# Attention in an inference step: where the value product stands among the transposes

## The chip, the cores and the metric

The kernel runs on one NeuronCore of a Trainium2 chip. The metric is the device time of one execution in microseconds (us), the median of the runs shown. The engines that matter are TensorE (PE in the profile; its weight loads are PEld), VectorE (DVE), ScalarE (ACT), GpSimd (POOL) and SyncE (SP), which issues transfers.

## What is computed

The reference is one step of a layer: modulated RMS norm, one projection into three head groups, their output projection, and a mixture of 16 experts. The change concerns the third head group, latent attention. Cut to that:

```python
q = jnp.einsum('bnr,rf->bnf', rmsnorm(c_q, q_norm_g), w_qb)      # 8 heads of 64 + 32
k, v = mla_keys_values(all_ckv, all_krope, w_kvb)                # k: 96 wide, v: 64 wide
s  = jnp.einsum('bqhd,bkhd->bhqk', qi, k).astype(jnp.float32) * ATTN_SCALE
pr = jax.nn.softmax(s, axis=-1).astype(v.dtype)
o  = jnp.einsum('bhqk,bkhd->bqhd', pr, v)
```

There are 1024 sample tokens, whose 8 query tiles of 128 see 1280 keys (1024 of their own and 256 cached), and 128 prompt tokens, one query tile that sees 128 keys. Everything is float32.

## The kernel before, in words

The program is written by hand, engine by engine, with semaphores; no scheduler moves anything. Attention takes 4 rounds, `i` = 0 to 3, of two heads each. The first three rounds are one loop body, the last is written out again with other filling work.

In a round, a **job** `n` is one head's 128 queries: token tile `t = n // 2`, head `j = n % 2` of the round. Jobs 0 to 15 have 1280 keys, jobs 16 and 17 (the prompt) 128. A job with an even number is called an even query here, the one behind it the odd query of the same tile. A job passes these steps:

- `score(i, n, ch)` (L711, TensorE): three matmuls, for 512, 512 and 256 keys, into PSUM banks 0 to 2 for an even job and 3 to 5 for an odd one. The first waits for `exp_ok` of job `n - 2`, which had the same banks.
- `highest` (L1554, VectorE): the maximum over the 1280 scores, and behind it the negated maximum (L1556).
- `exponential` (L1222, ScalarE): the exponential into `prob[n % 2]`, with its sum.
- `scaled` (L1575 and L1577, VectorE): reciprocal of the sum, and the row scaled by it. It posts `norm_ok`.
- `turn(n, ch)` (L753, TensorE): transposes of the probabilities, 4, 4 and 2 tiles of 128 for `ch` = 0, 1, 2, into PSUM banks 6 and 7 in turn. The first waits for `norm_ok`.
- `turned` (L1210 on ScalarE; L1588 on VectorE for chunk 0 of odd jobs, the list `DVE_TURNS`): these banks copied into `probT`.
- `weigh(t)` (L768, TensorE): the value product of both heads of tile `t`, 20 matmuls with an output of 64 rows each. It needs all chunks of `probT` of job `2t + 1`.
- `weighed` (L1568, VectorE): its result copied out. It posts `pv_out`.

TensorE's order is the Python loop in `attend` (two jobs to a step of `n`, called a **period** in this document). VectorE's order in a period is `highest(n)`, `turned(n - 1)`, `highest(n + 1)`, `scaled(n)`, `weighed((n - 2) // 2)`, `scaled(n + 1)`; in three periods of each of the first three rounds (`n` = 4, 6, 8) `fold_wq` (L1398, L1402) follows, a third of the next round's query weights each time. ScalarE's order is `turned(n - 2, 2)`, `exponential(n)`, `turned(n - 1, 1)`, `turned(n - 1, 2)`, `exponential(n + 1)`, `turned(n, 0)`, `turned(n, 1)`.

Banks 6 and 7 go round by the list `MID_ORDER`, which must name the turns and the value products in TensorE's order: entry number `at` uses bank `6 + at % 2`, and `bank_free` makes each wait until the entry two places before it is copied out. After job 15, the tail of a round mixes the last turns with `fill(x)`: the next round's `queries` (L681), or in the last round `out_proj` (L821).

Behind a round come the next two heads' keys and values (`keys_values`: L722, L694), and behind attention the rest of the output projection, the router and the experts (L1058, L1082), which take more than half of the time.

Of the kernel before, what the change touches and what calls it, by code (L numbers as in the profile page):

```python
# [131 lines left out]
def build(nc, x_prompt, x_sample, cache_ckv, cache_krope, c, c_ctx, w_ada, b_ada, norm1_g, norm2_g,  # L132
# [9 lines left out]
    with ctx:  # L142
# [232 lines left out]
        def pv_at(t):  # L375
            return bank[MID_BANK[("weigh", t)]][:, 0:P]

        def turn_out(eng, i, n, ch):

            if (n, ch) in DVE_TURNS:  # L380
                eng.wait_ge(t_out_d, i * len(DVE_TURNS) + DVE_TURNS.index((n, ch)) + 1)
            else:
                eng.wait_ge(t_out, i * len(ACT_TURNS) + ACT_TURNS.index((n, ch)) + 1)
# [148 lines left out]
        def _(pe):  # L532
# [22 lines left out]
            for n, job in enumerate(JOBS):  # L555
# [75 lines left out]
                elif kind == "gate":  # L631

                    m, g = job[1], job[2]
# [8 lines left out]
                elif kind == "pool":  # L642
                    m, g = job[1], job[2]
# [54 lines left out]
            def score(i, n, ch):  # L698

                t, j = divmod(n, 2)  # L700
                if n == 0:
                    pe.wait_ge(k_out, i * 3 + ch + 1)
                if n == 1 and ch == 0:
                    pe.wait_ge(q_out, i * 6 + 6)
                if n >= 2 and ch == 0:
                    pe.wait_ge(exp_ok, i * 18 + n - 1)
                if t < NT - 1:
                    k0, kn = ((0, 512), (512, 512), (1024, 256))[ch]
                else:
                    k0, kn = KEYS, NPR  # L710
                mm = pe.matmul(bank[3 * (n % 2) + ch][:, 0:kn], qT[:, j, t * P:(t + 1) * P], kT[:, j, k0:k0 + kn],  # L711
                               start=True, stop=True)
                if ch == 2 or t == NT - 1:
                    mm.then_inc(s_mm, 1)
# [19 lines left out]
            def attend(i, fill):  # L734

                def bank_free(user):

                    at = MID_ORDER.index(user)
                    if at < 2:
                        pe.wait_ge(v_out, i * 3 + 2 + at)  # L740
                    elif MID_ORDER[at - 2][0] == "turn":
                        turn_out(pe, i, *MID_ORDER[at - 2][1:])
                    else:
                        pe.wait_ge(pv_out, i * NT + MID_ORDER[at - 2][1] + 1)

                def turn(n, ch):

                    if ch == 0:
                        pe.wait_ge(norm_ok, i * 18 + n + 1)
                    bank_free(("turn", n, ch))  # L750
                    for a in range(CHUNK_TILES[ch] if n < 16 else 1):
                        kt = 4 * ch + a
                        mm = pe.transpose(bank[MID_BANK[("turn", n, ch)]][:, a * P:(a + 1) * P],  # L753
                                          prob[n % 2][:, kt * P:(kt + 1) * P], ident)
                    mm.then_inc(t_mm, 1)

                def weigh(t):

                    if t < 7:
                        turn_out(pe, i, 2 * t + 1, 0)  # L760
                    turn_out(pe, i, 2 * t + 1, 1 if t < NT - 1 else 0)
                    bank_free(("weigh", t))
                    for kt in range(10) if t < NT - 1 else range(10, 11):
                        if kt == 8:
                            turn_out(pe, i, 2 * t + 1, 2)
                        for j in range(2):
                            src = kt if t < NT - 1 else 0
                            mm = pe.matmul(pv_at(t)[64 * j:64 * j + 64, :], v_sb[:, kt, 64 * j:64 * j + 64],  # L768
                                           probT[:, 2 * (t % 2) + j, src * P:(src + 1) * P],
                                           start=(kt in (0, 10)), stop=(kt in (9, 10)))  # L770
                    mm.then_inc(pv_mm, 1)

                for n in range(2, 16, 2):
                    if n >= 4:
                        weigh((n - 4) // 2)
                    score(i, n, 0)
                    score(i, n, 1)
                    turn(n - 2, 0)
                    score(i, n, 2)
                    turn(n - 2, 1)  # L780
                    turn(n - 2, 2)
                    for ch in range(3):
                        score(i, n + 1, ch)
                        turn(n - 1, ch)
                weigh(6)
                score(i, 16, 0)
                fill(0)
                turn(14, 0)
                turn(14, 1)
                score(i, 17, 0)  # L790
                fill(1)
                turn(14, 2)
                turn(15, 0)
                fill(2)
                turn(15, 1)
                turn(15, 2)
                fill(3)
                turn(16, 0)
                turn(17, 0)
                weigh(7)  # L800
                fill(4)
                weigh(8)
                fill(5)
# [25 lines left out]
            with pe.Fori(0, 3) as i:  # L829
                attend(i, lambda x: queries(i + 1, x))  # L830
                keys_values(i + 1)
            attend(3, lambda x: out_proj(x) if x < 4 else None)


# [1299 lines left out]
def turns_before(n, ch):  # L2134
# [4 lines left out]
DVE_TURNS = [(n, 0) for n in range(1, 15, 2)]  # L2139
ACT_TURNS = [(n, ch) for n in range(18) for ch in range(3 if n < 16 else 1) if (n, ch) not in DVE_TURNS]  # L2140

MID_ORDER = [u for n in range(0, 14, 2) for u in [("weigh", (n - 2) // 2)][:n // 2]
             + [("turn", m, ch) for m in (n, n + 1) for ch in range(3)]]
MID_ORDER += [("weigh", 6)] + [("turn", n, ch) for n in (14, 15) for ch in range(3)]
MID_ORDER += [("turn", 16, 0), ("turn", 17, 0), ("weigh", 7), ("weigh", 8)]
MID_BANK = {u: 6 + at % 2 for at, u in enumerate(MID_ORDER)}

# [30 lines left out]
```

## Time and profile before

| | |
|---|---|
| median of 3 runs | 1656.54 us (1655.87 to 1659.05) |
| the profiled execution's own time | 1657.21 us |
| its span | 1655.2 us |
| PE busy | 1586.8 us (96%) |
| PEld busy | 1265.9 us (76%) |
| DVE busy | 551.5 us (33%) |
| ACT busy | 416.2 us (25%) |
| mean granted TensorE clock | 0.989 |

The span is what the profiler saw on the core; the execution's own time is 2.0 us longer, and the profiled execution was 0.7 us above the median. Matmuls are pipelined: the records of one group overlap, and the time a group takes is read from the start of one group to the start of the next. A float32 matmul leaves two records, a transpose one.

### The profile page before, as it was taken

How to read it: one execution, taken by the hardware profiler on the slowest of the kernel's cores; microseconds unless marked ns; L12 is line 12 of the kernel's file. 1: busy time of each engine (PE TensorE's matmuls, PEld its weight loads, DVE VectorE, ACT ScalarE, POOL GpSimd, SP SyncE). 2: the span in 40 equal slices, each digit the busy share in tenths (PEclk: the TensorE clock that was granted, in tenths of full speed). 3: DMA queues.
4: the chain of work that ended last, by engine and by line, in shares of the span. 5: the costliest groups of instructions: out<-in, count | busy, mean ns of one | idle time of the engine just before them, and what ended most of it. 6: DMA issues, size and time to landing. Idle time of an engine off the chain costs nothing.

```text
span 1655.2 us, 26952 instructions
## 1 busy us (share of the span) xinstructions
PE 1586.8 (96%) x10945; PEld 1265.9 (76%) x10945; DVE 551.5 (33%) x1315; ACT 416.2 (25%) x944; POOL 107.6 (7%) x109
## 2 busy tenths in 40 slices
PE   4899998999999999999879999999999999999997
PEld 3645444666667666544469999999999999999996
DVE  3101333474746646214477111111111111111114
ACT  4200101354545545233411111111111111111114
POOL 0004400000000000021100100000000000000010
PEclk9999999999999999999979999999999999999999
DMA  7861002200000000061149777878777878777776
GB/s 303 327 240 72 0 0 95 72 1 12 2 0 13 0 5 1 3 242 62 77 142 365 271 271 287 288 271 303 257 270 276 310 259 301 269 274 265 282 229 242
DMA packets 113514, 288.05 MB, mean 174 GB/s; under 512 B 10095, under 2 KB 15126, under 8 KB 110254
## 3 DMA queue, kind: packets, MB, share of 16 engines
q1 hardware_dynamic: 108702, 269.88, 44.3%
q0 software_dynamic: 4752, 17.30, 3.9%
q8 instruction: 45, 0.74, 0.2%
q14 instruction: 15, 0.12, 0.0%
HBM read 265.53 MB, written 21.64 MB: 174 GB/s over the span
## 4 chain that ended last, share of the span: by engine, by line
PE 94%; DVE 3%; DMA 1%; ACT 1%; issue 1%; SPq 0%; DVEq 0%
PE ps L1058 30%; PE ps L1082 15%; PE ps L711 9%; PE ps L537 9%; PE ps L821 7%; PE ps L768 5%; PE ps L753 4%; PE ps L681 3%; PE ps L598 2%; PE ps L694 1%; PE ps L722 1%; PE ps L550 1%; DVE hreg L1714 1%; PE ps L629 1%; PE ps L1013 1%; PE ps L1021 1%
## 5 line engine op out<-in xcount | busy, mean ns | idle before, releaser
L1058 PE MATMUL ps<-mreg,wreg 128*128 128x144 f32 x4096 | 517.9, 287 | 0.0
L1058 PEld LDWEIGHTS ps<-mreg,wreg 128*128 128x128 f32 x4096 | 509.7, 190 | 0.5 <-issue 0.4
L1082 PE MATMUL ps<-mreg,wreg 128*128 128x144 f32 x2048 | 265.5, 286 | 0.0
L1082 PEld LDWEIGHTS ps<-mreg,wreg 128*128 128x128 f32 x2048 | 258.0, 190 | 0.0
L1919 DVE TENSOR_TENSOR mreg<-ps,mreg 128x144 f32<-128x144 f32 x120 | 36.9, 307 | 443.0 <-PE ps L1058 443.0
L711 PE MATMUL ps<-wreg 128*128 128x512 f32 (+2 forms) x400 | 167.9, 519 | 0.0
L1344 ACT ACTIVATE mreg<-ps 128x144 f32<-128x144 f32 x128 | 37.1, 290 | 445.7 <-PE ps L1058 445.7
L537 PE MATMUL ps<-hreg,wreg 128*128 128x512 f32 (+1 forms) x432 | 143.2, 489 | 0.0
L821 PE MATMUL ps<-wreg,mreg 128*128 128x512 f32 x288 | 130.4, 598 | 2.6 <-DVE wreg L1635 2.6
L1554 DVE TENSOR_REDUCE stat<-ps 128x1 f32<-128x1280 f32 (+1 forms) x72 | 97.7, 1357 | 90.9 <-PE ps L711 90.9
L753 PEld LDWEIGHTS ps<-const,hreg 128*128 128x128 f32 x648 | 80.0, 141 | 58.3 <-issue 38.9
L537 PEld LDWEIGHTS ps<-hreg,wreg 128*128 128x128 f32 x432 | 70.7, 191 | 70.0 <-issue 69.6
L1210 ACT ACTIVATE hreg<-ps 128x512 f32<-128x512 f32 (+2 forms) x172 | 82.1, 501 | 109.9 <-PE ps L753 107.7
L1894 DVE TENSOR_SCALAR mreg<-ps,gain,modT 128x128 f32<-128x128 f32 x128 | 51.8, 408 | 160.2 <-PE ps L1013 160.0
L1222 ACT ACTIVATE hreg<-ps,stat 128x1280 f32<-128x1280 f32 (+1 forms) x72 | 88.0, 1222 | 68.3 <-DVE stat L1556 68.3
L1348 ACT ACTIVATE mreg<-ps,modT 128x128 f32<-128x128 f32 x128 | 47.0, 367 | 224.7 <-PE ps L1082 224.6
L753 PE MATMUL ps<-const,hreg 128*128 128x128 f32 x648 | 97.2, 274 | 0.0
L821 PEld LDWEIGHTS ps<-wreg,mreg 128*128 128x128 f32 x288 | 52.1, 190 | 57.8 <-issue 57.8
L711 PEld LDWEIGHTS ps<-wreg 128*128 128x128 f32 x400 | 64.0, 190 | 26.9 <-issue 24.9
L768 PE MATMUL ps<-hreg,wreg 128*64 128x128 f32 x1296 | 78.5, 275 | 4.6 <-ACT hreg L1210 1.1
L768 PEld LDWEIGHTS ps<-hreg,wreg 128*64 128x64 f32 x1296 | 70.9, 137 | 13.7 <-ACT hreg L1210 9.1
L1577 DVE TENSOR_SCALAR hreg<-hreg,stat 128x1280 f32<-128x1280 f32 (+1 forms) x72 | 59.0, 820 | 2.5
(254 smaller groups left out, 1174.1 us busy)
## 6 DMA issues: line engine op xcount, KB each, us to landing
wreg<-in_w_e_dram SPq DMA_DIRECT2D x96, 2048.0 KB, 12.2
wreg<-in_w_ada_dram SPq DMA_DIRECT2D x24, 1024.0 KB, 10.1
out_dram<-wreg SPq DMA_DIRECT2D x9, 512.0 KB, 2.6
mreg<-in_x_sample_dram SPq DMA_DIRECT2D x8, 512.0 KB, 8.3
wreg<-in_w_out_dram SPq DMA_DIRECT2D x1, 4096.0 KB, 13.4
wreg<-in_x_sample_dram SPq DMA_DIRECT2D x8, 512.0 KB, 6.0
x_rows<-wreg SPq DMA_DIRECT2D x8, 512.0 KB, 2.8
xn_rows<-wreg SPq DMA_DIRECT2D x8, 512.0 KB, 2.7
```

The costliest lines, as they stand in the source:

```text
L537: mm = pe.matmul(bank[n % 8][:, 0:gn], w_in_sb[:, k, w_at + m * P:w_at + (m + 1) * P], hT[:, k, g0:g0 + gn], start=(k == 0), stop=(k == KD ...
L711: mm = pe.matmul(bank[3 * (n % 2) + ch][:, 0:kn], qT[:, j, t * P:(t + 1) * P], kT[:, j, k0:k0 + kn], start=True, stop=True)
L753: mm = pe.transpose(bank[MID_BANK[("turn", n, ch)]][:, a * P:(a + 1) * P], prob[n % 2][:, kt * P:(kt + 1) * P], ident)
L768: mm = pe.matmul(pv_at(t)[64 * j:64 * j + 64, :], v_sb[:, kt, 64 * j:64 * j + 64], probT[:, 2 * (t % 2) + j, src * P:(src + 1) * P], start ...
L821: mm = pe.matmul(bank[o_bank(x)], mixT[:, k, t * P:(t + 1) * P], w_out_sb[:, k, hf * 512:(hf + 1) * 512], start=(k == 0), stop=(k == KD - 1))
L1058: mm = pe.matmul(o[:, 0:CAP], w[s][:, k, (f % 4) * P:(f % 4 + 1) * P], xsT[b][:, k, :], start=(k == 0), stop=(k == KD - 1))
L1082: mm = pe.matmul(bank[4 + dm % 2][:, 0:CAP], w2[f // 4][:, f % 4, dm * P:(dm + 1) * P], hidT[:, f, :], start=(f == 0), stop=(f == 7))
L1210: act.activation(probT[:, 2 * (t % 2) + j, ch * 512:ch * 512 + w], bank[MID_BANK[("turn", n, ch)]][:, 0:w], ACT.Copy).then_inc(t_out, 1)
L1222: act.activation(prob[n % 2][:, 0:w], src, ACT.Exp, bias=a_neg[:, n % 4:n % 4 + 1], scale=SCALE, accum_out=a_sum[:, n % 4:n % 4 + 1]).then ...
L1554: dve.tensor_reduce(a_max[:, r:r + 1], src, AX_X, ALU.max).then_inc(max_ok, 1)
L1577: dve.tensor_scalar(prob[n % 2][:, 0:w], prob[n % 2][:, 0:w], a_rec[:, r:r + 1], None, ALU.mult).then_inc(norm_ok, 1)
L1894: dve.tensor_scalar(xsT[b][:, k, 0:CAPS], bank[6 + k % 2][:, 0:CAPS], gain2[:, 0, k:k + 1], modT[:, 0, 24 + k:25 + k], ALU.mult, ALU.add). ...
```

## The change

Two places change together. In TensorE's loop, `weigh` moves from ahead of a period's scores to behind `score(i, n, 2)`, so that it stands after chunk 0 of the even query's transposes and ahead of chunks 1 and 2. The last one, `weigh(6)`, moves from ahead of `score(i, 16, 0)` to behind `turn(14, 0)`. `MID_ORDER` follows, so the bank of each entry and the entry it waits for change too. The orders of VectorE, ScalarE, GpSimd and SyncE do not change.

```diff
                 for n in range(2, 16, 2):
-                    if n >= 4:
-                        weigh((n - 4) // 2)
                     score(i, n, 0)
                     score(i, n, 1)
                     turn(n - 2, 0)
                     score(i, n, 2)
+                    if n >= 4:
+                        weigh((n - 4) // 2)
                     turn(n - 2, 1)
                     turn(n - 2, 2)
                     for ch in range(3):
                         score(i, n + 1, ch)
                         turn(n - 1, ch)
-                weigh(6)
                 score(i, 16, 0)
                 fill(0)
                 turn(14, 0)
+                weigh(6)
                 turn(14, 1)
...
-MID_ORDER = [u for n in range(0, 14, 2) for u in [("weigh", (n - 2) // 2)][:n // 2]
-             + [("turn", m, ch) for m in (n, n + 1) for ch in range(3)]]
-MID_ORDER += [("weigh", 6)] + [("turn", n, ch) for n in (14, 15) for ch in range(3)]
+MID_ORDER = [u for n in range(0, 16, 2)
+             for u in [("turn", n, 0)] + [("weigh", (n - 2) // 2)][:n // 2] + [("turn", n, 1), ("turn", n, 2)]
+             + [("turn", n + 1, ch) for ch in range(3)]]
```

TensorE, one period of the last round, before. L768 is the value product, L711 the scores, L753 the transposes:

```order
350 L768 MATMUL ps<-hreg,wreg 64x128 x20
351 L711 MATMUL ps<-wreg 128x512 x2
352 L753 MATMUL ps<-const,hreg 128x128 x4
353 L711 MATMUL ps<-wreg 128x256
354 L753 MATMUL ps<-const,hreg 128x128 x6
355 L711 MATMUL ps<-wreg 128x512
356 L753 MATMUL ps<-const,hreg 128x128 x4
357 L711 MATMUL ps<-wreg 128x512
358 L753 MATMUL ps<-const,hreg 128x128 x4
359 L711 MATMUL ps<-wreg 128x256
360 L753 MATMUL ps<-const,hreg 128x128 x2
```

and the same period now:

```order
343 L711 MATMUL ps<-wreg 128x512 x2
344 L753 MATMUL ps<-const,hreg 128x128 x4
345 L711 MATMUL ps<-wreg 128x256
346 L768 MATMUL ps<-hreg,wreg 64x128 x20
347 L753 MATMUL ps<-const,hreg 128x128 x6
348 L711 MATMUL ps<-wreg 128x512
349 L753 MATMUL ps<-const,hreg 128x128 x4
350 L711 MATMUL ps<-wreg 128x512
351 L753 MATMUL ps<-const,hreg 128x128 x4
352 L711 MATMUL ps<-wreg 128x256
353 L753 MATMUL ps<-const,hreg 128x128 x2
```

The 20 matmuls of the value product have passed three score matmuls and the four transposes of the even query's chunk 0; nothing else has changed places.

TensorE, the tail of the last round (L821 is the output projection that fills there), as the difference:

```order
 L711 MATMUL ps<-wreg 128x128
 L821 MATMUL ps<-wreg,mreg 128x512 x8
-L753 MATMUL ps<-const,hreg 128x128 x8
+L753 MATMUL ps<-const,hreg 128x128 x4
+L768 MATMUL ps<-hreg,wreg 64x128 x20
+L753 MATMUL ps<-const,hreg 128x128 x4
 L711 MATMUL ps<-wreg 128x128
 L821 MATMUL ps<-wreg,mreg 128x512 x8
```

`weigh(6)` now stands between the two chunks of job 14, behind a whole piece of filling work.

VectorE, one period of the last round, which is the same before and now (L1554 and L1556 are `highest`, L1588 `turned`, L1575 and L1577 `scaled`, L1568 `weighed`; in the first three rounds `fold_wq` follows in three periods):

```order
273 L1554 TENSOR_REDUCE stat<-ps 128x1
274 L1556 TENSOR_SCALAR stat<-stat 128x1
275 L1588 COPY hreg<-ps 128x512
276 L1554 TENSOR_REDUCE stat<-ps 128x1
277 L1556 TENSOR_SCALAR stat<-stat 128x1
278 L1575 RECIPROCAL stat<-stat 128x1
279 L1577 TENSOR_SCALAR hreg<-hreg,stat 128x1280
280 L1568 COPY mreg<-ps 128x128
281 L1575 RECIPROCAL stat<-stat 128x1
282 L1577 TENSOR_SCALAR hreg<-hreg,stat 128x1280
```

The copy of the value product (L1568) stays where it was, between the scaling of the even query and that of the odd one.

## Rows read from the trace of the kernel before

**Rows 1.** The page: busy time and instructions of each engine, and the chain's engines.

```profile
PE 1586.8 (96%) x10945; PEld 1265.9 (76%) x10945; DVE 551.5 (33%) x1315; ACT 416.2 (25%) x944; POOL 107.6 (7%) x109
...
PE 94%; DVE 3%; DMA 1%; ACT 1%; issue 1%; SPq 0%; DVEq 0%
```

**Rows 2.** Timeline of PE, one period: start us, us, what [idle before]; later pieces left out.

```profile
338.39 0.38 PE L753 MATMUL ps<-const,hreg 128*128 128x128 f32 x2
338.90 2.40 PE L768 MATMUL ps<-hreg,wreg 128*64 128x128 f32 x40
341.23 1.98 PE L711 MATMUL ps<-wreg 128*128 128x512 f32 x4
343.06 0.60 PE L753 MATMUL ps<-const,hreg 128*128 128x128 f32 x4
...
343.93 0.85 PE L753 MATMUL ps<-const,hreg 128*128 128x128 f32 x6
344.62 1.02 PE L711 MATMUL ps<-wreg 128*128 128x512 f32 x2
...
347.64 0.38 PE L753 MATMUL ps<-const,hreg 128*128 128x128 f32 x2
```

**Rows 3.** Windows of one period: length, busy us of PE, PEld, DVE, ACT, POOL, clock, DMA.

```profile
338.90:348.15 9.25, 9.13 (x72) 6.43 (x73) 6.80 (x14) 5.28 (x10) 0.00 (x0) 1.00 0.01 2
```

**Rows 4.** Line 768: what it waited for and who waited for it (us, times).

```profile
  ACT hreg L1210: 10.2, 29
...
  DVE mreg L1568: 19.2, 25
```

**Rows 5.** Timeline of PEld, the value product's weight loads in the same period.

```profile
338.87 2.19 PEld L768 LDWEIGHTS ps<-hreg,wreg 128*64 128x64 f32 x40 [0.33 <-ACT hreg L1210]
```

**Rows 6.** Timeline of ACT in the same period.

```profile
338.16 1.03 ACT L1210 ACTIVATE hreg<-ps 128x512 f32<-128x512 f32 x2 [0.15 <-PE ps L753]
340.31 1.33 ACT L1222 ACTIVATE hreg<-ps,stat 128x1280 f32<-128x1280 f32 x1 [1.11 <-DVE stat L1556]
341.53 0.19 ACT L1222 ACTIVATION_READ_ACCUMULATOR hreg<-ps,stat 128x1 f32 x1
343.69 0.60 ACT L1210 ACTIVATE hreg<-ps 128x512 f32<-128x512 f32 x1 [1.97 <-PE ps L753]
```

**Rows 7.** Timeline of DVE in the same period.

```profile
338.59 1.49 DVE L1554 TENSOR_REDUCE stat<-ps 128x1 f32<-128x1280 f32 x1 [1.04 <-PE ps L711]
...
340.19 0.15 DVE L1575 RECIPROCAL stat<-stat 128x1 f32<-128x1 f32 x1
340.38 0.89 DVE L1577 TENSOR_SCALAR hreg<-hreg,stat 128x1280 f32<-128x1280 f32 x1
341.45 0.29 DVE L1568 COPY mreg<-ps 128x128 f32 x1 [0.18 <-PE ps L768]
341.76 0.16 DVE L1575 RECIPROCAL stat<-stat 128x1 f32<-128x1 f32 x1
341.95 0.89 DVE L1577 TENSOR_SCALAR hreg<-hreg,stat 128x1280 f32<-128x1280 f32 x1
342.76 0.32 DVE L1398 TENSOR_SCALAR hreg<-hreg,vT 128x192 f32<-128x192 f32 x1
342.99 0.38 DVE L1402 TENSOR_SCALAR hreg<-hreg,vT 128x32 f32<-128x32 f32 x2
344.13 1.49 DVE L1554 TENSOR_REDUCE stat<-ps 128x1 f32<-128x1280 f32 x1 [0.76 <-PE ps L711]
...
346.11 0.69 DVE L1588 COPY hreg<-ps 128x512 f32<-128x512 f32 x1 [0.31 <-PE ps L753]
```

**Rows 8.** Timeline of PE ahead of attention: a piece behind a long wait.

```profile
282.64 0.76 PE L653 MATMUL ps<-const,wreg 128*128 128x128 f32 x4 [2.34 <-DVE wreg L1516]
```

**Rows 9.** Windows, the columns as in rows 3, PEclk behind POOL's.

```profile
280.00:290.00 10.00, 6.47 (x16) 3.27 (x16) 5.26 (x17) 2.88 (x7) 0.00 (x0) 0.66 0.96 344
700.00:710.00 10.00, 7.40 (x46) 4.08 (x42) 4.57 (x14) 2.63 (x4) 4.66 (x2) 1.00 0.71 259
```

## Prediction

> **What bounds the kernel now.** I read the page first: TensorE is busy 96% of the span, and 94% of the chain that ended last lies on it [rows 1]. So what TensorE waits for counts one for one, and what the others wait for costs nothing until TensorE waits for them. Next the timeline of one period of attention on TensorE. The value product starts at 338.90 and again at 348.15, 9.25 us later [rows 2, 3]. Inside a period the pieces start one behind the other, with one hole: the last two transposes of the odd query start at 338.39 and stream for 0.23 us (six take 343.93 to 344.62, 0.69 us), so TensorE is free at 338.62, and the value product starts at 338.90. That is 0.28 us. The waits of its line say for what: ScalarE's copies, 29 times, 10.2 us in all, 0.35 us each [rows 4]. The copy of chunk 1 starts at 338.16 and takes 0.60 us, to 338.76, and the weight load follows at 338.87 [rows 5, 6]. So a result is handed to TensorE in 0.11 us.
>
> Then VectorE over the same period. It is busy 6.80 of 9.25 us [rows 3], never late, and its order is fixed. `highest` of the odd query starts at 338.59, 0.20 us behind the start of the transposes at 338.39; `scaled` of the even query ends at 340.38 + 0.89 = 341.27; the value product's copy runs at 341.45, with only 0.18 us of waiting ahead of it; `scaled` of the odd query follows, then `fold_wq` to 342.99 + 0.38 = 343.37 [rows 7]. All of this lies behind the 2.33 us of the value product and the 1.83 us of the two scores behind it (338.90, 341.23, 343.06) [rows 2]. The even query's probabilities are ready at 341.27 and first transposed at 343.06: 1.79 us of room, less 0.11.
>
> **The change, step by step.** No instruction is added or removed; no transfer moves. TensorE gets three score matmuls and four transposes ahead of the value product, and the place of VectorE's copy of it stays.
>
> *What is saved.* The 0.28 us hole: between the odd query's last transposes and the value product lie now at least 1.83 + 0.87 us of work (341.23 to 343.06, then 343.06 to 343.93) [rows 2], and ScalarE is done in 0.5. Over 7 value products in 4 rounds this is 28 x 0.28 = 7.8 us, if nothing else happens.
>
> *What is added first.* The even query's transposes now come 2.33 us sooner after the odd scores. TensorE, free at 338.62, would start the two scores at once and end them at 338.62 + 1.83 = 340.45, while the probabilities come at 341.27 + 0.11 = 341.38. It waits 0.93 us. Net of the hole: +0.65.
>
> *What is added next, and is larger.* VectorE takes things in order, and the copy of the value product stands ahead of `scaled` of the odd query and of `highest` of the next even query. Before, it waited 0.18 us for that product. Now the product cannot start before the transposes of chunk 0, which cannot start before `scaled` of the even query. VectorE has to stand idle for 0.11 + 0.87 (chunk 0 and the third score) + 2.55 (product start 338.90 to copy start 341.45) = 3.53 us from its own `scaled` to its own copy, where it stood 0.18. Its idle time in a period was only 9.25 - 6.80 = 2.45 us, so it becomes a part of the loop that sets the period. Two closed loops result; each is a sum of steps from [rows 2, 7].
>
> Loop A, with `fold_wq`, lies on VectorE but for the product: `highest` to the next instruction 1.60 (338.59 to 340.19), `turned` 0.69, `highest` of the odd query 1.60, reciprocal and scaling of the even one 1.08 (340.19 to 341.27), hand-over 0.11, transposes and third score 0.87, product up to its copy 2.55, copy 0.31 (341.45 to 341.76), scaling of the odd one 1.00 (to 342.76), folding 0.61 (to 343.37). Sum **10.42 us**. Without the folding it is 9.81, and the other loop rules.
>
> Loop B goes through TensorE: product 2.55, copy 0.29 and hand-over 0.11 (chunk 2 of the even query takes the product's bank and waits for its copy), two transposes 0.23, the odd query's scores with the transposes between them 3.02 (344.62 to 347.64), 0.20 to `highest`, 1.60, 1.08, 0.11, 0.87. Sum **10.06 us**.
>
> Against 9.25 that is +1.17 us in a period with folding and +0.81 without. ScalarE's exponential of the even query, 3.13 us from `highest` to its end (338.59 to 341.53 + 0.19, the same for both) [rows 6, 7], also comes late, and the next scores wait some 0.6 us for it; but the transposes behind them wait for VectorE anyway, so the wait only takes part of theirs.
>
> *The sum.* A round has 7 large value products. Its first full period pays the +0.65 above; five intervals between products follow, three of them with folding in rounds 0 to 2: 3 x 1.17 + 2 x 0.81 = 5.13. At the tail, job 16's scores wait about 0.6 us for job 14's exponential, less the hole of 0.28 and some overlap: I take +0.25, an estimate between 0 and 0.6. The filling projections there hide the rest. Round: 5.13 + 0.65 + 0.25 = 6.03. The last round does not fold: 5 x 0.81 + 0.90 = 4.95. Sum 3 x 6.03 + 4.95 = **23.0 us**. On the profiled execution's 1657.2 us this gives 1680.2; that execution was 0.7 above the median, so I say **1679.5 us**, 1.4% slower.
>
> *Bounds.* From below: back to back, VectorE's instructions overlap by 0.08 us (342.76 against 341.95 + 0.89), which could shorten each of the eight steps of loop A a little, to 9.9, where loop B holds it; then all periods cost 0.81 less some hundredths and the sum is near 17. From above: each hand-over to TensorE may expose twice the 0.11, one more in loop A and two in loop B, 28 x 0.2 = 6 us, and the tail may pay all of its 0.6, 1.4 us more: 30.
>
> **A rule weighed.** In the period, weight loads fill 6.43 of 9.25 us, 70%, and VectorE 6.80, 74% [rows 3]: by these shares neither is full. The Trainium skill, "Perfetto Trace Analysis", section "Identifying the Most-Contended Engine", says to judge TensorE's headroom by the weight loads' share rather than by matmul busy time, and VectorE's by its share. By that reading both have a quarter to spare, the order would not matter and the sum would be zero. I take the starts of the pieces instead, since they follow each other with 0.28 us free in 9.25.
>
> **The rivals.**
>
> 1. *Faster.* The hole goes and nothing takes its place. This needs the even query's probabilities on TensorE's side at 340.45 at the latest in the time of the rows, 0.93 us sooner than they come; from there on the sign turns. Then 28 x 0.28 = 7.8 us go: 1648.7. For it: VectorE idles 2.45 us in a period. Against: the idle time lies ahead of steps that need TensorE's scores, not where it could be used. 0.05.
> 2. *No change.* The slack of VectorE (2.45 us) takes in the added wait, and TensorE's hole and wait cancel: within 3 us of 1656.5. The rule above is its best argument; the closed loops speak against it, since they leave no slack. 0.04.
> 3. *Waits in series.* The late exponential (0.6 us) is not absorbed but adds to the loop, each period: 28 x 0.6 = 17 on top of 23, so 1696. It would need chunk 0's transposes to follow the scores without waiting. 0.08.
> 4. *The clock falls.* Before attention, TensorE waited 2.34 us in one piece [rows 8], and in these 10 us its granted clock was 0.66, so part of them ran at the lower of its two levels (1.2 and 2.4 GHz). But in 700 to 710 it was busy only 7.40 us of 10 at 1.00, and a forecast period is busy at least 8.5 of 10 [rows 9]. If every period ran at 0.66, 34% of some 290 us would come on top, about 98: near 1777. The Trainium skill, "TensorE: Matmul & The Clock Gate", section "A second HAM failure mode: psum-queue depth-cycling", describes just such short idle times between groups of matmuls setting the clock back and forth. 0.02.
>
> My forecast has 0.81.
>
> **How the numbers follow.** The forecast's own range is 1656.5 + 17 - 2 for small things not seen, to 1656.5 + 30 + 3: 1671 to 1690. Rivals 1, 2 and 4 and most of 3 lie outside, 0.19, so the range of 8 in 10 is just this one. A measurement of this kernel can tell about 0.2%, 3.3 us, from no change. Faster takes rival 1, 0.05; same rival 2, 0.04; slower the rest, 0.91.
>
> **What would show it.** Right: value products 10.4 us apart in the folding periods, 10.06 in others; about 3.5 us of idle time ahead of each copy on line 1568, so that its wait for line 768 grows from 19.2 us [rows 4] to near 100; TensorE's line 753 waiting for VectorE's line 1577 and for the product's copy, line 711 for ScalarE's line 1222; the wait of line 768 for ScalarE down from 10.2 us to about 1; the clock at 1.00; everything behind attention unchanged in length. Wrong: products 9.0 us apart (rival 1) or 9.25 (rival 2); a wait of 0.6 us ahead of the scores with a full 1 us still ahead of the transposes (rival 3); a granted clock below 1.00 between 310 and 730 us (rival 4).

## The result and the profile after

The changed kernel takes **1682.32 us** (median of 4 runs, 1681.56 to 1684.86), the kernel before 1657.36 (4 runs, 1655.87 to 1659.05). The ratio is 1.0153, with a 95% interval of 1.0141 to 1.0165: 1.5% slower, 25 us. The forecast was 1679.5, between 1671 and 1690.

The page of the changed kernel, to be held against [rows 1]:

```profile
PE 1598.5 (95%) x10945; PEld 1258.8 (75%) x10945; DVE 543.9 (32%) x1315; ACT 411.9 (25%) x944; POOL 107.8 (6%) x109
...
PE 88%; DVE 8%; issue 2%; DMA 1%; ACT 1%; SPq 0%; DVEq 0%; ACTq 0%
```

The instructions are as many as before, and TensorE is about as busy. What moved is the chain: 94% on TensorE has become 88%, and VectorE has gone from 3% to 8%. VectorE, busy a third of the span, is now in part what the end waits for.

All of the loss is in attention. I call **attention** the stretch from the first matmul on line 722 (the first round's keys) to the end of the last value product. It goes from 300.59 to 724.68 + 2.62 = 727.30 us, which is 426.71 us, by the changed kernel's timeline of PE:

```profile
300.59 0.59 PE L722 MATMUL ps<-creg,share 128*128 128x512 f32 x1
...
724.68 2.62 PE L768 MATMUL ps<-hreg,wreg 128*64 128x128 f32 x44 [0.35 <-ACT hreg L1210]
```

The same two places of the kernel before lie at 299.64 and 701.69: 402.05 us. The difference is 24.66. Behind attention it is 953.50 us against 953.51.

The waits of line 768 and those of the two engines it feeds. First who waited for the value product, and for whom it waited, against [rows 4]:

```profile
  issue: 10.9, 31
  ACT hreg L1210: 3.2, 8
who waited for it (us, times):
  DVE mreg L1568: 122.8, 32
```

VectorE's copy now waits 122.8 us for it instead of 19.2. And the waits of attention, 310 to 730 us (engine and line, whom it waited for: us, times, longest):

```profile
PEld ps L711 <- ACT hreg L1222: 14.3, 24, 0.6
...
PEld ps L753 <- DVE hreg L1577: 10.0, 12, 1.7
PE ps L711 <- ACT hreg L1222: 8.6, 24, 0.4
PEld ps L753 <- DVE hreg L1588: 6.6, 13, 0.7
PE ps L753 <- DVE hreg L1577: 6.4, 15, 0.9
...
PEld ps L753 <- DVE mreg L1568: 2.5, 16, 0.2
```

None of these waits stood there before: scores for the exponential, transposes for the scaled probabilities, for `turned`, and for the value product's copy. One period with folding on TensorE, from product to product (345.43 to 355.73, 10.30 us, where [rows 2, 3] have 9.25):

```profile
345.43 2.40 PE L768 MATMUL ps<-hreg,wreg 128*64 128x128 f32 x40
347.76 1.01 PE L753 MATMUL ps<-const,hreg 128*128 128x128 f32 x6
348.61 1.02 PE L711 MATMUL ps<-wreg 128*128 128x512 f32 x2
...
352.07 0.44 PE L753 MATMUL ps<-const,hreg 128*128 128x128 f32 x2 [0.27 <-DVE hreg L1588]
352.88 1.98 PE L711 MATMUL ps<-wreg 128*128 128x512 f32 x4 [0.38 <-ACT hreg L1222]
354.72 0.65 PE L753 MATMUL ps<-const,hreg 128*128 128x128 f32 x4
...
355.73 2.40 PE L768 MATMUL ps<-hreg,wreg 128*64 128x128 f32 x40
```

and on VectorE, against [rows 7]:

```profile
339.39 1.49 DVE L1554 TENSOR_REDUCE stat<-ps 128x1 f32<-128x1280 f32 x1
...
341.01 0.69 DVE L1588 COPY hreg<-ps 128x512 f32<-128x512 f32 x1
341.62 1.48 DVE L1554 TENSOR_REDUCE stat<-ps 128x1 f32<-128x1280 f32 x1
...
343.21 0.15 DVE L1575 RECIPROCAL stat<-stat 128x1 f32<-128x1 f32 x1
343.39 0.89 DVE L1577 TENSOR_SCALAR hreg<-hreg,stat 128x1280 f32<-128x1280 f32 x1
347.98 0.29 DVE L1568 COPY mreg<-ps 128x128 f32 x1 [3.70 <-PE ps L768]
348.19 0.15 DVE L1575 RECIPROCAL stat<-stat 128x1 f32<-128x1 f32 x1
348.38 0.89 DVE L1577 TENSOR_SCALAR hreg<-hreg,stat 128x1280 f32<-128x1280 f32 x1
349.18 0.32 DVE L1398 TENSOR_SCALAR hreg<-hreg,vT 128x192 f32<-128x192 f32 x1
...
349.70 1.48 DVE L1554 TENSOR_REDUCE stat<-ps 128x1 f32<-128x1280 f32 x1
```

The reader should see loop A here: VectorE goes from `highest` at 339.39 to `highest` at 349.70 without one idle moment of its own but the 3.70 us ahead of the copy. Before, a folding period had waits for scores of 0.76 and 1.04 us. From `highest` of the even query to the transposes a second way of equal length runs beside VectorE's: through ScalarE's exponential and the scores that wait for it (`<-ACT hreg L1222` above). e11 shows what follows from that.

### The profile page after: what moved, and what is told of

The parts are those of the page before. It is cut to its first block, busy times and chain, and to the rows that moved or that the text cites. A ratio compares the mean times of both kernels' runs of the same rounds, so it can differ in the third digit from the quotient of the medians.

```text
span 1680.8 us, 26931 instructions
## 1 busy us (share of the span) xinstructions
PE 1598.5 (95%) x10945; PEld 1258.8 (75%) x10945; DVE 543.9 (32%) x1315; ACT 411.9 (25%) x944; POOL 107.8 (6%) x109
## 4 chain that ended last, share of the span: by engine, by line
PE 88%; DVE 8%; issue 2%; DMA 1%; ACT 1%; SPq 0%; DVEq 0%; ACTq 0%
PE ps L1058 30%; PE ps L1082 14%; PE ps L537 8%; PE ps L821 7%; PE ps L711 5%; PE ps L768 5%; PE ps L753 3%; PE ps L681 3%; DVE stat L1554 2%; PE ps L598 2%; PE ps L694 1%; PE ps L722 1%; PE ps L550 1%; DVE hreg L1714 1%; PE ps L629 1%
## 5 line engine op out<-in xcount | busy, mean ns | idle before, releaser
L711 PE MATMUL ps<-wreg 128*128 128x512 f32 (+2 forms) x400 | 167.5, 518 | 8.6 <-ACT hreg L1222 8.6
L753 PEld LDWEIGHTS ps<-const,hreg 128*128 128x128 f32 x648 | 73.6, 141 | 81.5 <-issue 46.2
L821 PE MATMUL ps<-wreg,mreg 128*128 128x512 f32 x288 | 130.4, 598 | 2.6 <-DVE wreg L1635 2.6
L753 PE MATMUL ps<-const,hreg 128*128 128x128 f32 x648 | 103.1, 280 | 8.8 <-DVE hreg L1577 6.4
L1554 DVE TENSOR_REDUCE stat<-ps 128x1 f32<-128x1280 f32 (+1 forms) x72 | 97.4, 1353 | 37.5 <-PE ps L711 37.5
L1222 ACT ACTIVATE hreg<-ps,stat 128x1280 f32<-128x1280 f32 (+1 forms) x72 | 87.9, 1221 | 81.1 <-DVE stat L1556 80.7
L821 PEld LDWEIGHTS ps<-wreg,mreg 128*128 128x128 f32 x288 | 52.1, 190 | 57.8 <-issue 57.8
L711 PEld LDWEIGHTS ps<-wreg 128*128 128x128 f32 x400 | 64.0, 190 | 36.4 <-issue 20.1
L768 PEld LDWEIGHTS ps<-hreg,wreg 128*64 128x64 f32 x1296 | 70.0, 137 | 12.9 <-issue 10.9
L768 PE MATMUL ps<-hreg,wreg 128*64 128x128 f32 x1296 | 78.5, 275 | 1.1 <-ACT hreg L1210 1.1
L1577 DVE TENSOR_SCALAR hreg<-hreg,stat 128x1280 f32<-128x1280 f32 (+1 forms) x72 | 59.0, 820 | 2.6
## 6 DMA issues: line engine op xcount, KB each, us to landing
wreg<-in_w_ada_dram SPq DMA_DIRECT2D x24, 1024.0 KB, 10.3
```

The costliest lines, as they stand in the source:

```text
L821: mm = pe.matmul(bank[o_bank(x)], mixT[:, k, t * P:(t + 1) * P], w_out_sb[:, k, hf * 512:(hf + 1) * 512], start=(k == 0), stop=(k == KD - 1))
L1222: act.activation(prob[n % 2][:, 0:w], src, ACT.Exp, bias=a_neg[:, n % 4:n % 4 + 1], scale=SCALE, accum_out=a_sum[:, n % 4:n % 4 + 1]).then ...
L1554: dve.tensor_reduce(a_max[:, r:r + 1], src, AX_X, ALU.max).then_inc(max_ok, 1)
L1577: dve.tensor_scalar(prob[n % 2][:, 0:w], prob[n % 2][:, 0:w], a_rec[:, r:r + 1], None, ALU.mult).then_inc(norm_ok, 1)
```

## The experiments

Eleven kernels were run, each beside runs of the kernel before on its own chip (medians 1657.11 us for e1 to e4, 1657.75 for e5 to e8, 1657.06 for e9 to e11). The table has the two measures: the whole (ratio to the kernel before, with its interval) and attention alone, from the profile of each kernel. Attention is the sharper one. The stretch ahead of it, which no edit touches, ended between 297.7 and 303.4 us in the profiles, and a spread of that size is in the totals too; behind attention the profiles have 952.6 to 955.2 us (e8 apart). Attention came out at 402.05, 402.04 and 402.09 us in the three kernels whose TensorE order is that of the kernel before.

| kernel | median us | ratio | attention us | to before | products apart, us: without folding / with / last round |
|---|---|---|---|---|---|
| before | 1657.36 | | 402.05 | | 9.25 / 9.25 / 9.25 |
| after | 1682.32 | 1.0153 (1.0141 to 1.0165) | 426.71 | +24.66 | 10.25 / 10.31 / 10.05 |
| e1_first_score | 1654.10 | 0.9984 (0.9976 to 0.9993) | 397.39 | -4.66 | 9.06 / 9.06 / 9.06 |
| e2_tail_only | 1660.01 | 1.0012 (1.0003 to 1.0020) | 401.20 | -0.85 | 9.25 / 9.25 / 9.25 |
| e3_vector_order | 1656.12 | 0.9990 (0.9981 to 0.9999) | 398.37 | -3.68 | 9.12 / 9.25 / 9.01 |
| e4_copy_later | 1679.14 | 1.0135 (1.0120 to 1.0149) | 423.64 | +21.59 | 10.24 / 10.23 / 10.05 |
| e5_two_scores | 1656.72 | 0.9993 (0.9984 to 1.0002) | 399.62 | -2.43 | 9.01 / 9.37 / 9.01 |
| e6_after_more_vector | 1685.26 | 1.0162 (1.0147 to 1.0178) | 429.77 | +27.72 | 10.25 / 10.65 / 10.05 |
| e7_before_more_vector | 1658.04 | 0.9999 (0.9989 to 1.0008) | 402.04 | -0.01 | 9.25 / 9.25 / 9.25 |
| e8_after_unrolled | 1731.21 | 1.0445 (1.0430 to 1.0459) | 425.70 | +23.65 | 10.17 / 10.24 / 10.05 |
| e9_before_vector_order | 1658.02 | 1.0006 (0.9996 to 1.0015) | 402.09 | +0.04 | 9.25 / 9.25 / 9.25 |
| e10_first_score_and_tail | 1652.54 | 0.9978 (0.9968 to 0.9988) | 396.57 | -5.48 | 9.06 / 9.06 / 9.06 |
| e11_scaled_first | 1673.64 | 1.0098 (1.0082 to 1.0113) | 416.46 | +14.41 | 9.73 / 10.25 / 9.61 |

**Half of the change's way.** The value product behind one score matmul, where nothing of the even query's transposes is passed:

```diff
                 for n in range(2, 16, 2):
-                    if n >= 4:
-                        weigh((n - 4) // 2)
                     score(i, n, 0)
+                    if n >= 4:
+                        weigh((n - 4) // 2)
                     score(i, n, 1)
                     turn(n - 2, 0)
```

> The kernel before, with the value product one score matmul later: behind score(i, n, 0) instead of ahead of it; the tail and the bank order stay. Theory (the loop through VectorE, entered because the even query's probabilities come too late): their scaling has room here, since the product and a score still lie ahead of the transposes, so only the 0.28 us hole goes: products 8.97 us apart, some 7 to 8 us off the whole, ratio 0.995. Rival A (any step of the value product away from its place costs on TensorE, by switching between kinds of matmul or by the bank order): same or slower than before. Rival B (only the late exponential matters): as the theory here.

The products stand 9.06 us apart and attention is 4.66 us shorter, so rival A falls: moving the product does not by itself make the kernel slower. Of the hole of 0.28 us, 0.19 came back as time. The timeline of PE shows the rest:

```profile
334.37 1.02 PE L711 MATMUL ps<-wreg 128*128 128x512 f32 x2
335.23 0.60 PE L753 MATMUL ps<-const,hreg 128*128 128x128 f32 x4
...
336.10 0.38 PE L753 MATMUL ps<-const,hreg 128*128 128x128 f32 x2
336.32 1.02 PE L711 MATMUL ps<-wreg 128*128 128x512 f32 x2
337.27 2.40 PE L768 MATMUL ps<-hreg,wreg 128*64 128x128 f32 x40
339.61 1.12 PE L711 MATMUL ps<-wreg 128*128 128x512 f32 x2
340.57 0.60 PE L753 MATMUL ps<-const,hreg 128*128 128x128 f32 x4
```

The scores follow the transposes at once (336.32), but the product starts 0.95 us behind the start of a score that streams for 0.86 elsewhere (334.37 to 335.23), and the score behind the product takes 0.96 (339.61 to 340.57). The steps from score to product and from product to score cost some 0.1 us each here, and the first of them is new. That is also why less came than was expected: six products of a round move here, not seven, and 24 x 0.19 = 4.6 us. The median gained 3.0 us of the 7 to 8 that were expected.

**The tail alone.** The loop and its banks as before; only this, and the last entries of `MID_ORDER` in step:

```diff
-                weigh(6)
                 score(i, 16, 0)
                 fill(0)
                 turn(14, 0)
+                weigh(6)
                 turn(14, 1)
```

> Only the second half of the change: weigh(6) behind turn(14, 0), the loop's periods as before. Theory: the tail has filling work of the next projections on TensorE, so nothing waits; one hole of 0.28 us a round goes, about -1 us in all, within the noise. Then the whole cost of the change is that of the loop. Rival (the tail carries a good part of the 25 us): +3 us or more.

Attention is 0.85 us shorter, as expected. The whole came out 0.12% longer, and its runs fell in two groups, three near 1656.5 and eight near 1660.5 us. The profiled one, of the second group, entered attention at 302.44 us, 2.80 later than the profiled run of the kernel before, and needed 1.7 us more behind it (955.2 against 953.5). Neither stretch was edited, and no experiment here explains why this kernel's runs are mostly the longer ones. The tail has no part in the 24.66 us.

**VectorE's order.** TensorE as in the change. On VectorE, this:

```diff
                     highest(i, n)
                     turned(n - 1)
+                    scaled(n)
                     highest(i, n + 1)
-                    scaled(n)
-                    weighed((n - 2) // 2)
                     scaled(n + 1)
+                    weighed((n - 2) // 2)
```

> The changed kernel, TensorE's order and banks as changed; VectorE's order alone is another: scaled(n) ahead of highest(n + 1), and the value product's copy behind scaled(n + 1). Theory: the even query's probabilities come 1.6 us sooner, and nothing of VectorE stands behind the product but its own copy, so both loops open: products about 9.0 us apart without folding and 9.3 with it, the whole 3 to 7 us faster than the kernel before, ratio 0.996 to 0.998. Rival A (the new place costs on TensorE itself, or by its banks): it stays 20 to 25 us slower. Rival B (the exponential's lateness sets the loop): in between, 10 us slower or more.

In attention the 24.66 us are gone and 3.68 with them; the whole is 1.0 us below the kernel before (0.9990), where 3 to 7 were expected. This is the strongest result: TensorE issues the very order of the changed kernel, so neither its order nor its banks make the loss by themselves. The last round of this kernel on VectorE:

```profile
617.19 0.89 DVE L1577 TENSOR_SCALAR hreg<-hreg,stat 128x1280 f32<-128x1280 f32 x1
617.99 1.49 DVE L1554 TENSOR_REDUCE stat<-ps 128x1 f32<-128x1280 f32 x1
...
621.35 0.89 DVE L1577 TENSOR_SCALAR hreg<-hreg,stat 128x1280 f32<-128x1280 f32 x1
622.63 0.29 DVE L1568 COPY mreg<-ps 128x128 f32<-128x128 f32 x1 [0.39 <-PE ps L768]
622.84 1.48 DVE L1554 TENSOR_REDUCE stat<-ps 128x1 f32<-128x1280 f32 x1
```

The even query is scaled at 617.19, ahead of the odd query's maximum, and the copy waits 0.39 us, where it waits 3.53 in the last round of the changed kernel. TensorE's products are 9.01 us apart.

**One half of it, the copy.** The changed kernel with only the value product's copy moved:

```diff
                     scaled(n)
-                    weighed((n - 2) // 2)
                     scaled(n + 1)
+                    weighed((n - 2) // 2)
```

> The changed kernel with half of that: only the value product's copy behind scaled(n + 1) on VectorE, highest(n + 1) still ahead of scaled(n). Theory: loop A (through VectorE's own order) opens and loop B (product, copy, bank, odd scores, highest, scaling of the even query, transposes) stays: products 10.05 us apart in folding periods too, +16 to +19 us to the kernel before, 6 to 9 less than the change. Rival (VectorE's stall ahead of the copy is all of it): near the time of the kernel before.

Products are 10.23 us apart in folding periods too: loop A is open, loop B stands. Attention is 3.1 us shorter than the change's, not 6 to 9, because loop B is longer in the looped rounds (10.23) than the 10.05 expected and found in the last one; e8 takes that up. Of the 3.1 us, 0.75 lie in the five intervals of the looped rounds (51.17 us a round instead of 51.42) and some 2.3 in the interval behind the sixth product (9.79 instead of 10.37). The rival falls: VectorE's stall ahead of the copy was not all of it.

**The other half.** The copy stays ahead of `scaled(n + 1)`:

```diff
+                    scaled(n)
                     highest(i, n + 1)
-                    scaled(n)
                     weighed((n - 2) // 2)
```

> The changed kernel with the other half of the VectorE edit alone: scaled(n) ahead of highest(n + 1), the value product's copy still ahead of scaled(n + 1). Theory: loop B opens (the probabilities no longer wait for the maximum of the odd query), loop A stays in another form, from the copy through scaled(n + 1), highest of the next even query, its exponential, its scaling, the transposes and the product: 9.7 to 9.9 us without folding and about 10.3 with it, +12 to +16 us to the kernel before. Rival (each half takes away its own share of the cost, so that they add): 21.6 of 24.7 us stay with the first half alone, so this one would have to end near the kernel before.

9.61 to 9.73 us without folding and 10.25 with it, +14.41: loop B is open, another form of loop A is left. It runs through ScalarE's exponential of the even query and the two scores behind it. In a folding period of this kernel the even query is scaled at 342.77 + 0.89 = 343.66, and the transposes start only at 344.41, behind scores that waited for the exponential:

```profile
342.59 1.98 PE L711 MATMUL ps<-wreg 128*128 128x512 f32 x4 [0.38 <-ACT hreg L1222]
344.41 0.60 PE L753 MATMUL ps<-const,hreg 128*128 128x128 f32 x4
```

So with folding the way through VectorE's own steps and the way through the exponential are nearly equal: taking the first away made the period only 0.06 us shorter (10.31 to 10.25). The late exponential, rival B of e3, is thus the second branch of loop A; e3 opens both, since from the product's end to the even query's `highest` only the copy and the folding are left there. The two halves take away 3.1 and 10.3 us of the change's cost alone, 28.3 together. They are two loops over the same period, and the period is as long as the longer one.

**VectorE's order with TensorE's old one.** The two moves of e3, made in the kernel before:

```diff
+                    scaled(n)
                     highest(i, n + 1)
-                    scaled(n)
-                    weighed((n - 2) // 2)
                     scaled(n + 1)
+                    weighed((n - 2) // 2)
```

> The kernel before with the VectorE order of the run that undid the cost (scaled(n) ahead of highest(n + 1), the copy behind scaled(n + 1)); TensorE as before. A control. Theory: with TensorE's old order no loop runs through VectorE, so this order is worth nothing by itself: products 9.25 us apart, attention within 0.5 us of the kernel before. Rival (that VectorE order is simply the better one, and its gain hid a cost of TensorE's new order): 4 us faster or more.

402.09 us, and the whole at 1.0006 of the kernel before. The order is worth nothing until a loop runs through it.

**More work for VectorE, in both kernels.** Behind each folding (the declaration of the spare tile is left out):

```diff
                         fold_wq(i + 1, range(n // 2 - 2, n // 2 - 1))
+                        for a, b in ((0, 192), (192, 224), (224, 256)):
+                            dve.tensor_scalar(spare[:, n // 2 - 2, a:b], raw_spare[:, a:b], SCALE, None, ALU.mult)
```

> The changed kernel with three extra small VectorE instructions (of the shapes of the weight folding, into a spare tile) behind each folding: 9 periods get about 0.52 us more of VectorE work. Theory: VectorE closes loop A, so each of these 9 periods is 0.5 us longer (10.33 to 10.85), +4 to +5 us to the change, and periods without folding stay. Rival (TensorE's own new order, or loop B alone, sets every period): no more than the 0.2 us of slack is passed on, under 2 us.

> The same extra VectorE work in the kernel before. Theory: VectorE waits 0.76 us for the next scores there, so 0.52 us more costs nothing: products 9.25 us apart everywhere, attention unchanged within 0.5 us. Rival (VectorE's work counts in either order): +4 to +5 us as well.

The three instructions took 0.34 us back to back, not 0.52. VectorE in the changed kernel with them, and then in the kernel before with them (the lines lie two further down):

```profile
341.57 0.43 DVE L1602 TENSOR_SCALAR spare<-g_rows 128x192 f32<-128x192 f32 x3
341.91 1.49 DVE L1556 TENSOR_REDUCE stat<-ps 128x1 f32<-128x1280 f32 x1
```

```profile
347.03 0.42 DVE L1602 TENSOR_SCALAR spare<-g_rows 128x192 f32<-128x192 f32 x3
347.87 1.49 DVE L1556 TENSOR_REDUCE stat<-ps 128x1 f32<-128x1280 f32 x1 [0.42 <-PE ps L713]
```

In the changed kernel `highest` starts right behind, and each folding period is 0.34 us longer (10.31 to 10.65); 9 of them make 3.06, and attention grew by just that, 426.71 to 429.77. In the kernel before, the wait for the scores shrank from 0.76 to 0.42 us and nothing else happened. The same work costs its full length in one order and nothing in the other.

**Two scores.** The kernel before with the value product just ahead of the even query's first transposes:

```diff
-                    if n >= 4:
-                        weigh((n - 4) // 2)
                     score(i, n, 0)
                     score(i, n, 1)
+                    if n >= 4:
+                        weigh((n - 4) // 2)
                     turn(n - 2, 0)
```

> The kernel before, with the value product behind two score matmuls but still ahead of the even query's first transposes; tail and bank order stay. Theory: the probabilities still come in time (needed 4.16 us behind the odd scores, ready after 2.76), so loop B does not form; VectorE's copy comes 0.8 us later than in the run behind one score, and in folding periods VectorE is then full: products 9.06 us apart without folding, 9.3 to 9.5 with it; attention within 4 us below to 2 us above the kernel before. Rival (the cost grows evenly with the number of scores that the product is moved behind): it lies half way to the change, +10 us.

Periods with folding take 9.37 us, others 9.01; attention is 2.43 us below the kernel before. With one place further, past four transposes and a small score, it is 24.66 above. The cost is not proportional to the way: it sets in where the product passes the transposes that wait for VectorE. A place between these transposes and the small score was not tried, so that the transposes and not the score make the difference rests on the waits of the trace.

**TensorE without its loop.** In the changed kernel:

```diff
-            with pe.Fori(0, 3) as i:
+            for i in range(3):
                 attend(i, lambda x: queries(i + 1, x))
```

> The changed kernel with TensorE's first three rounds written out instead of looped, so that TensorE has no register instructions ahead of its waits; order, banks and all other engines stay. In the changed kernel products without folding between them are 10.25 us apart in the looped rounds and 10.05 in the written-out last one. Theory: the 0.2 us are TensorE's register instructions, hidden while TensorE runs ahead of its waits and laid bare by the new waits: 10.05 us in all rounds without folding, folding periods between 10.1 and 10.3, 1 to 4 us less in all. Rival (the loops of VectorE or ScalarE, or the folding's wake, make it): 10.25 stays.

Inside attention it gave 10.17 us instead of 10.25, so TensorE's register instructions explain 0.08 of the 0.20 us, not all; "10.05 in all rounds" was wrong. They stand between the end of VectorE's scaling and the transposes: 0.13 us in the looped rounds of the changed kernel, 0.05 in its last round and in e8. The rest, 0.12 to 0.13, lies on VectorE, between the product's start and its copy. The timeline of DVE in the changed kernel has in a looped round

```profile
327.43 0.29 DVE L1568 COPY mreg<-ps 128x128 f32 x1 [3.72 <-PE ps L768]
```

behind a product that started at 324.85, 2.58 us; and in the last round

```profile
646.67 0.29 DVE L1568 COPY mreg<-ps 128x128 f32<-128x128 f32 x1 [3.53 <-PE ps L768]
```

behind one that started at 644.22, 2.45 us. The rows of line 1568 name what stands ahead of it in the looped rounds alone:

```profile
L1568 DVEq FUSED_REGOPS  x27: 57/57/81, 327.3 to 609.3; - x27
```

The address of its output is worked out from the loop's register there. No run took VectorE's loop away, so for these 0.13 us the starts are the evidence. Other kernels have the same step: 2.58 us in the looped rounds of e8, whose TensorE has no loop, and 2.55 looped against 2.44 in the last round of the kernel before.

The rest of e8 is a surprise: the kernel took 1731 us, and 49.5 of the 73 us above the kernel before lie behind attention, where not one instruction of the program was edited. It is told below.

**The two gains together.** The edits of e1 and e2 in one kernel, with the banks in step:

```diff
                     score(i, n, 0)
+                    if n >= 4:
+                        weigh((n - 4) // 2)
                     score(i, n, 1)
...
                 fill(0)
                 turn(14, 0)
+                weigh(6)
                 turn(14, 1)
```

> The two edits that each shortened attention together: the value product behind the first score matmul in the loop, and weigh(6) behind turn(14, 0). Theory: the gains of 4.7 and 0.9 us lie in different places and add: attention 396.2 to 397 us against 402.05, the whole 0.996 to 0.998 of the kernel before. Rival (the tail's gain was one of the loop's last hole, which is gone already): as with the first edit alone, 397.4.

They add: 396.57 us, 5.48 below the kernel before (4.66 + 0.85 = 5.51). The whole is 1652.54 us, ratio 0.9978 (0.9968 to 0.9988), the lowest median of this study.

## Why the prediction was right

The direction, the place and the mechanism were as forecast, and the size within 2.8 us of the median. That the size fits owes something to luck, since one term is 0.15 us too small in every period and others are too large. Point by point:

- *The hole of 0.28 us goes.* It did: line 768 waited for ScalarE 8 times and 3.2 us, after 29 and 10.2. I had said about 1 us; the eight left (four on PE, four on PEld) are at `weigh(7)` in each round's tail, which the change does not move.
- *The first transposes wait 0.93 us.* In round 0 TensorE waited 0.90 us at that place.
- *VectorE idles 3.53 us ahead of its copy.* It was 3.70 in the looped rounds: 0.13 for the hand-over, 1.02 for chunk 0 and the third score, 2.55 from product to copy, where I had 0.11, 0.87 and 2.55. The 3.53 of the last round are 0.05, 1.02 and 2.45, so that the figure agrees there is luck.
- *Loop A is 10.42 us.* It is 10.31. One term was too small: chunk 0 and the third score up to the product took 1.02 us (344.41 to 345.43), not 0.87, in every period of the change. I had read 0.87 where transposes follow the third score; a product behind it starts 0.53 us after the score's start instead of 0.44, the same step that e1 shows, and the transposes ahead of it took 0.49 instead of 0.43. The way from the even query's reciprocal to the copy took 4.77 us (343.21 to 347.98) where my terms make 4.61, and nearly all of the difference is this step. Others were too large: `turned` to the next `highest` took 0.61 instead of 0.69 and folding 0.52 (349.18 to 349.70) instead of 0.61, since a duration holds an end that overlaps with the next instruction's start. The copy took 0.21 instead of 0.31 up to the reciprocal: before, that reciprocal still waited for ScalarE's sum (341.53 + 0.19 = 341.72, start at 341.76), which now lies long behind.
- *Loop B is 10.06 us.* It is 10.05 in the last round and 10.25 in the looped ones. The 0.19 us of the looped rounds are mostly the same term: 1.01 instead of 0.87. The register instructions were in my terms already, since I took 2.55 and 0.11 from a looped round, which now has 2.58 and 0.13. In the last round product to copy is 2.45 and the hand-over 0.05, which makes up for the 1.02: that 10.06 fits there is luck.
- *Five intervals of a folding round cost 5.13 us.* Measured 5.16 in round 0 (51.42 against 46.26): the two misses cancel. The last round's five cost 4.00, forecast 4.05.
- *The first period and the tail cost 0.90 a round.* Here lies most of what was missed. The rest of a round is 1.34 us in the looped rounds and 1.15 in the last: from the first score to the first product it took 10.33 us where the kernel before would need 9.52 (6.82 and the 2.70 of scores and transposes now ahead), 0.8 instead of my 0.65, again by the 1.01 for 0.87; and the tail took some 0.5 instead of 0.25.
- *The exponential's wait is absorbed.* In a period without folding it is 0.34 us ahead of the scores, and the transposes behind them still wait 0.29 for VectorE; rival 3 wanted 0.6 and a full 1. With folding it is 0.38, and the transposes then do not wait at all. There it is absorbed by no margin: the scores start at 342.57 and take 1.83, to 344.40, and VectorE's hand-over ends at 344.41. My own terms have the same tie, 5.07 us from `highest` through the exponential (3.13, 0.11, 1.83) and 5.08 through VectorE, and I did not say so. A slightly later exponential would have set the period.
- *The lower bound of 17 us.* It does not follow from my terms: 20 intervals at 0.81 and 4 x 0.90 make 19.8.
- *The clock.* It stayed at 1.00 through attention, as in this window of one period of the changed kernel (the columns as in [rows 3]):

```profile
335.10:345.43 10.33, 9.68 (x74) 6.10 (x73) 6.47 (x13) 5.07 (x10) 0.00 (x0) 1.00 0.00 0
```

Several waits of 0.3 to 0.4 us in a period did not bring it down. The Trainium skill ("TensorE: Matmul & The Clock Gate", section "A second HAM failure mode: psum-queue depth-cycling") describes short idle times that do; this trace has none of it: the clock is 1.00 throughout attention.

The same row speaks to the rule that was weighed. Weight loads fill 59% of this period and VectorE 63%, less than before, and yet the period is 1.08 us longer. By the Trainium skill's "Identifying the Most-Contended Engine" (in "Perfetto Trace Analysis") headroom on both engines has grown. The trace does not disagree with the shares; it shows that they say nothing of a loop in which each engine waits for the other.

## What to carry to other kernels

When a step of the busiest engine is moved by a fraction of a microsecond's gain, look at what stands behind its result in the in-order queue of the other engines: a copy that waited 0.18 us and then waits 3.70 takes everything behind it along, and an engine busy a third of the time can close the loop. Write the period as closed loops (each step's start to the next one's start, not durations) for the old and the new order, and take the longest; moving the product up to, but not past, the transposes that wait for VectorE shortened attention by 2.4 to 4.7 us, moving it past them lengthened it by 24.7. If a move of one engine's order does not pay, the matching move of the other's may be what is missing: here it was worth 28 us.

## What the runs showed of the hardware that was not expected

**Register instructions appear when a wait does.** In looped rounds with addresses and semaphore values worked out in registers, the kernel before ran at the same 9.25 us a period as in the written-out last round. Once waits closed the loop, looped periods took 10.25 us and written-out ones 10.05. At VectorE's copy the time was there before as well (2.55 us from the product's start, against 2.44 written out) and cost nothing, since VectorE had idle time to spare.

**Writing out a loop slowed a later one.** e8 has TensorE's three rounds written out, and what lies behind attention, unchanged, took 49.5 us more: 1002.99 us against 953.50 in the changed kernel. The waits of TensorE in that kernel, and its queue that brings instructions, show where:

```profile
PE ps L1058 <- issue: 29.5, 10, 3.3
```

```profile
q8 instruction: 100, 1.64, 0.4%
```

That queue moved 100 packets, 45 before, and at ten places of the experts' loop TensorE stood still for about 3 us, released by nothing that the profile shows, for example here:

```profile
1236.21 2.30 PE L1058 MATMUL ps<-mreg,wreg 128*128 128x144 f32 x11 [3.15 <-issue]
1241.29 5.20 PE L1058 MATMUL ps<-mreg,wreg 128*128 128x144 f32 x21 [2.77 <-issue]
```

The packets fit the stalls. From 1115 to 1614 us, inside the experts' loop, that queue moved nothing in the changed kernel, and in e8

```profile
q8 instruction: 43, 0.70, 0.6%
```

The ten stalls come in five pairs, one to a turn of the loop, 105 to 108 us apart, and at each of them a packet of this queue starts within 0.8 us (stalls from 1128.04 and 1134.20, packets at 1128.1 and 1134.3). So in the changed kernel the loop ran without bringing in instructions, and in e8 they were brought in again at each turn. The clock adds to it: from 1100 to 1650 us the mean granted clock was 0.96, in the kernel before and the changed one 1.00, and over its whole span TensorE was busy 18.3 us longer with the same instructions (1616.8 against 1598.5). With the 29.5 us of stalls this is nearly all of the 49.5. Why the written-out rounds ahead of the loop bring this about was not tried and stays open.
